# Forget attention: the softmax division moved from the probabilities into the output gate

## What is computed

```python
def fox_mixer(h, w_in, b_f, g_q, g_k, w_out):
    q, k, v, z, f_logit = jnp.split(h @ w_in, [FOX_AD, 2 * FOX_AD, 3 * FOX_AD, 4 * FOX_AD], axis=-1)
    q, k = rms_norm(q per head, g_q), rms_norm(k per head, g_k)
    F = jnp.cumsum(log_sigmoid(f_logit + b_f), axis=1)
    for i in range(S // BLK):                      # 4 blocks of 128 queries
        s = einsum('bhqd,bhkd->bhqk', q[:, :, lo:hi], k[:, :, :hi]) * scale
        s = s + F[:, :, lo:hi, None] - F[:, :, None, :hi]
        p = softmax(where(causal, s, -inf), axis=-1)
        outs.append(einsum('bhqk,bhkd->bhqd', p, v[:, :, :hi]))
    o = concatenate(outs, axis=2)
    return (o * silu(z)) @ w_out
```

## Time and profile before

| | |
|---|---|
| time, median of 3 runs | 2850.07 us (2848.01 to 2853.19) |
| span of the profiled execution | 2851.4 us |
| TensorE busy | 2608.8 us (91%) |
| VectorE busy | 1410.3 us (49%) |
| ScalarE busy | 1064.9 us (37%) |
| attention loop of the forget attention | from 788.2 to 887.2 us of the span |
| mean granted TensorE clock | 0.949 of full speed |

### The profile page before, as it was taken

How to read it: one execution, slowest core, us unless ns; L and a number is a source line. 1 busy time by engine, 2 the same in 40 slices (tenths; PEclk the granted TensorE clock), 3 DMA queues, 4 the chain that set the end, 5 groups by cost and what they waited for, 6 DMA issues and landing times.

```text
span 2851.4 us, 33398 instructions
## 1 busy us (share of the span) xinstructions
PE 2608.8 (91%) x13262; PEld 2117.5 (74%) x13262; DVE 1410.3 (49%) x2386; ACT 1064.9 (37%) x1871; POOL 269.3 (9%) x420
## 2 busy tenths in 40 slices
PE   6889899999889989999869999999967999999998
PEld 4677777788446777787647888878845888888887
DVE  4667566554374656552244333235844665533322
ACT  3355432332353545453434222233253443322222
POOL 5233021011000023000000000001001110000000
PEclk9999999999899999999879999999987999999999
DMA  5522274265111412141102333333310000233332
GB/s 213 184 71 81 86 242 157 75 199 170 53 38 54 141 30 60 60 122 52 45 30 67 104 97 97 94 94 107 90 52 1 1 1 1 67 111 97 96 96 74
DMA packets 146229, 250.19 MB, mean 88 GB/s; under 512 B 15455, under 2 KB 65914, under 8 KB 145049
## 3 DMA queue, kind: packets, MB, share of 16 engines
q1 hardware_dynamic: 129008, 198.08, 22.2%
q0 software_dynamic: 14816, 48.31, 5.1%
q10 hardware_dynamic: 2249, 1.65, 0.2%
HBM read 245.84 MB, written 5.30 MB: 88 GB/s over the span
## 4 chain that ended last, share of the span: by engine, by line
PE 77%; ACT 8%; DVE 8%; DMA 4%; issue 2%; POOL 0%; SPq 0%; DVEq 0%; ACTq 0%
PE PS L218 20%; PE PS L219 19%; PE PS L220 19%; PE PS L985 2%; ACT tmp L752 1%; PE PS L2313 1%; PE PS L2316 1%; DMA hT_b<-in_w_mod 1%; DVE x L808 1%; PE PS L2323 1%; PE PS L1760 1%; PE PS L2326 1%; PE PS L1445 1%; ACT w_hi L203 1%; PE PS L1744 1%
## 5 line engine op out<-in xcount | busy, mean ns | idle before, releaser
L210 DVE TENSOR_TENSOR w_lo<-w_raw,w_hi 128x1024 fp32r<-128x1024 f32 (+1 forms) x344 | 412.4, 1206 | 783.5 <-ACT w_hi L203 782.3
L203 ACT ACTIVATE w_hi<-w_raw 128x1024 fp32r<-128x1024 f32 (+1 forms) x344 | 356.8, 1045 | 1041.4 <-DMA w_raw<-in_ffn_w_gate_up 311.8
L218 PE MATMUL PS<-hT_hi,w_hi 128*128 128x512 f32 (+1 forms) x1728 | 662.6, 383 | 20.8 <-DVE hT_lo L820 12.7
L219 PE MATMUL PS<-hT_lo,w_hi 128*128 128x512 f32 (+1 forms) x1728 | 654.0, 378 | 0.0
L220 PE MATMUL PS<-hT_hi,w_lo 128*128 128x512 f32 (+1 forms) x1728 | 653.6, 378 | 0.0
L218 PEld LDWEIGHTS PS<-hT_hi,w_hi 128*128 128x128 f32 x1728 | 332.0, 192 | 84.7 <-issue 17.5
L220 PEld LDWEIGHTS PS<-hT_hi,w_lo 128*128 128x128 f32 x1728 | 331.9, 192 | 59.6
L219 PEld LDWEIGHTS PS<-hT_lo,w_hi 128*128 128x128 f32 x1728 | 332.5, 192 | 56.2 <-issue 0.2
L218 PE MATMUL PS<-w_hi,hT_hi 128*128 128x512 f32 (+1 forms) x704 | 290.3, 412 | 31.3 <-ACT gla_szT L1054 8.2
L219 PE MATMUL PS<-w_lo,hT_hi 128*128 128x512 f32 (+1 forms) x704 | 279.0, 396 | 0.0
L220 PE MATMUL PS<-w_hi,hT_lo 128*128 128x512 f32 (+1 forms) x704 | 277.9, 395 | 0.0
(11 more groups left out here) (564 smaller groups left out, 3479.8 us busy)
## 6 DMA issues: line engine op xcount, KB each, us to landing
w_raw<-in_ffn_w_gate_up SPq DMA_DIRECT2D x176, 256.0 KB, 3.1
mraw<-in_w_mod POOLq DMA_DIRECT2D x160, 256.0 KB, 4.0
w_raw<-in_gla_w_in SPq DMA_DIRECT2D x48, 512.0 KB, 4.7
w_raw<-in_ffn_w_down SPq DMA_DIRECT2D x44, 512.0 KB, 3.7
w_raw<-in_fox_w_in SPq DMA_DIRECT2D x32, 512.0 KB, 4.2
w_raw<-in_sgu_w_in SPq DMA_DIRECT2D x24, 512.0 KB, 4.9
w_raw<-in_dn_w_in SPq DMA_DIRECT2D x24, 512.0 KB, 3.6
w_raw<-in_gla_w_out SPq DMA_DIRECT2D x16, 512.0 KB, 4.7
```

Source lines behind the costliest of these rows:

```text
L203: nc.scalar.activation(w_hi[:, n % NS, :, 0:m], w_raw[:, n % NS, :, 0:m], ACT.Copy).then_inc(w_hidone, 1)
L210: nc.vector.tensor_tensor(w_lo[:, n % NS, :, 0:m], w_raw[:, n % NS, :, 0:m], w_hi[:, n % NS, :, 0:m].bitcast(F32), ALU.subtract).then_inc( ...
L218: nc.tensor.matmul(o, l_hi, r_hi, start=start, stop=False)
L219: nc.tensor.matmul(o, l_hi, r_lo, start=False, stop=False)
```

## The change

The probabilities are no longer divided by their row sums. The exponential writes its row sums into `r.den`, a column for each of the pair's eight units. `scale` goes; `turn` waits for the exponential itself. After a pair's last exponential VectorE inverts all eight sums at once (`invert`). TensorE gets a new step `shares`: eight matmuls of a reciprocal column, broadcast to 64 columns, with the identity, which put the reciprocals of both heads as rows into bank 7. `gate` has a new first operation, which multiplies this bank into `r.szT`, and a new wait for `q.row`. `shares(k)` stands between `values` and `turn` in the step t = 1 of the next pair (u % 8 == 2), and `gate(k)` behind the reduction of the unit with u % 8 == 3, both for the pair before; the last pair's stand behind the loop. The semaphore `f1` is renamed `row`, and the counts of other layers that share `scl` are adapted.

```diff
                 def turn(u):
                     h, t = units[u]
-                    t_.wait_ge(q.scl, u + 1)
+                    t_.wait_ge(q.ex, u + 1)
...
+                def shares(k):
+                    t_.wait_ge(q.scl, k + 1)
+                    if k:
+                        t_.wait_ge(q.os, os_at + k)
+                    for t in range(TT):
+                        for e2 in range(2):
+                            at = 2 * t + e2
+                            mm = t_.matmul(PS[FD * e2:FD * e2 + FD, 7, t * P:(t + 1) * P],
+                                           r.rd[:, k % 2, at:at + 1].to_broadcast([P, FD]), ident[:], start=True, stop=True)
+                    mm.then_inc(q.row, 1)
+
                 scores(0)
                 for u in range(0, len(units) + 2, 2):
                     if u + 2 < len(units):
                         scores(u + 2)
                     if u >= 2:
                         values(u - 2)
+                    if u % 8 == 2 and u > 8:
+                        shares(u // 8 - 1)
                     if u < len(units):
                         turn(u)
                         turn(u + 1)
+                shares(NP - 1)
                 t_.wait_ge(q.os, os_at + KT)
...
-                    a.activation(p, p, ACT.Exp, scale=-1.0, bias=r.st[:, u % 3, 0:1], accum_out=r.st[:, u % 3, 1:2]).then_inc(q.ex, 1)
+                    a.activation(p, p, ACT.Exp, scale=-1.0, bias=r.st[:, u % 3, :],
+                                 accum_out=r.den[:, u // 8 % 2, u % 8:u % 8 + 1]).then_inc(q.ex, 1)
...
-                def scale(u):
-                    h, t = units[u]
-                    v.wait_ge(q.ex, u + 1)
-                    then_dve(v.reciprocal(r.st[:, u % 3, 2:3], r.st[:, u % 3, 1:2]))
-                    p = pb(u)[:, 0:(t + 1) * P]
-                    v.tensor_scalar(p, p, r.st[:, u % 3, 2:3], None, ALU.mult).then_inc(q.scl, 1)
-                    if t == TT - 1 and h % 2 and h >= 3:
-                        gate(h // 2 - 1)
+                def invert(k):
+                    v.wait_ge(q.ex, 8 * k + 8)
+                    v.reciprocal(r.rd[:, k % 2, :], r.den[:, k % 2, :]).then_inc(q.scl, 1)
 
                 def gate(k):
+                    v.wait_ge(q.row, k + 1)
+                    then_dve(v.tensor_tensor(r.szT[:, k, :], PS[:, 7, :], r.szT[:, k, :], ALU.mult))
                     v.wait_ge(q.pv, 2 * TT * (k + 1))
                     then_dve(v.tensor_tensor(hf[:, k % 2, :], PS[:, 5 + k % 2, :], r.szT[:, k, :], ALU.mult))
                     then_dve(v.tensor_copy(hT_hi[:, k, :], hf[:, k % 2, :]))
...
-                                           scalar=-NEG, op0=ALU.add, op1=ALU.min, accum_out=r.st[:, u % 3, 0:1]).then_inc(q.ttr, 1)
-                    if u >= 1:
-                        scale(u - 1)
-                scale(len(units) - 1)
+                                           scalar=-NEG, op0=ALU.add, op1=ALU.min, accum_out=r.st[:, u % 3, :]).then_inc(q.ttr, 1)
+                    if u % 8 == 1 and u > 8:
+                        invert(u // 8 - 1)
+                    if u % 8 == 3 and u > 8:
+                        gate(u // 8 - 1)
+                invert(NP - 1)
                 gate(NP - 1)
```

More of the change, by code:

```diff
@@ L1427, in program @@
         su = sig("su", "sc ttr ex scl pt pts pv po")
-        fox_s = sig("fox", "cols lz f1 F_done flat FR0 FR1 FR2 FR3 cm cmb bones")
+        fox_s = sig("fox", "cols lz row F_done flat FR0 FR1 FR2 FR3 cm cmb bones")
         def norm_heads(base, n_tiles, per, bank, banks, sums, sq, tile, gain, rows_at, spread):
@@ L1485, in fox_layer @@
                        mask=([P, P], BF16), unit=([P, P], BF16), sums=([P, 4 * FH],), gains=([P, 8],),
-                       st=([P, 3, 4],))
+                       st=([P, 3, 1],), den=([P, 2, 8],), rd=([P, 2, 8],))
             r.F = r.FR[0:FH, 3, :]
@@ L1661, in dve @@
                 then_dve(v.tensor_tensor(r.F, r.FR[0:FH, 0, :], r.F, ALU.subtract))
-                v.memset(r.FR[0:FH, 1, :], 1.0).then_inc(q.f1, 1)
-                v.wait_ge(q.f1, 1)
+                then_dve(v.memset(r.FR[0:FH, 1, :], 1.0))
                 v.tensor_tensor_scan(r.F, r.FR[0:FH, 1, :], r.F, 0.0, ALU.mult, ALU.add).then_inc(q.F_done, 1)
@@ L1914, in att_layer @@
             NU = len(units)
-            soft = softmax_units(units + mu, FH * TT, FH * TT, 0, Group(P=r.P, PT=r.PT, st=None))
+            soft = softmax_units(units + mu, FH * TT, FH // 2, 0, Group(P=r.P, PT=r.PT, st=None))
             FILL_AT = {}
@@ L2236, in dn_layer @@
             UN = FH * TT + AH * TT + 2 * MH * TT
-            B = Group(xm=UN, pc=UN, xe=UN, te=UN, tm=UN, ym=UN, ve=0, sd=FH * TT + 2 * MH * TT,
+            B = Group(xm=UN, pc=UN, xe=UN, te=UN, tm=UN, ym=UN, ve=0, sd=FH // 2 + 2 * MH * TT,
                                 rm=0, vm=0, sm=AH // 2, rr=AH // 2, os=KT * (DEPTH + 1), kte=0)
@@ L2280, in dn_layer @@
             mu = memory_units(m_)
-            mem = softmax_units(mu, FH * TT + AH * TT + MH * TT, FH * TT + MH * TT, 8, Group(P=m_.P, PT=m_.PT, st=None))
+            mem = softmax_units(mu, FH * TT + AH * TT + MH * TT, FH // 2 + MH * TT, 8, Group(P=m_.P, PT=m_.PT, st=None))
             def load():
```

## The result

| | before | after |
|---|---|---|
| time, median | 2849.04 us (4 runs, 2839.27 to 2853.19) | 2871.38 us (4 runs, 2868.53 to 2879.89) |
| ratio | | 1.0079, 95% interval 1.0051 to 1.0107 |
| span of the profiled execution | 2851.4 us | 2866.7 us |
| loop, first scores to output projection | 788.18 to 887.21, 99.0 us | 783.01 to 908.09, 125.1 us |
| VectorE busy | 1410.3 us | 1387.6 us |

A forecast was written before the change was run, and what follows sets the result against it. It took TensorE and VectorE as both near full in the loop, a pair taking 11.46 us. Seven longer pairs (20.1), the first pair (-0.7) and the end (+1.6) sum to +21.0 us, so 2871.1, range 2865 to 2881.

The forecast's parts named there:

- The hold: In the loop, `gate` waits for `shares` and delays the reduction that scores of t = 3 need: 2.87 us longer, seven pairs.
- Shares: On TensorE in step t = 1, sixteen records without free time: 0.88 us a pair, bounds 0.88 and 1.34.
- The gain of the scaling: Turns of t = 0 and t = 1 no longer wait for VectorE's scaling: 0.73 us a pair saved.
- The first pair: At the loop's start, the first pair has no gate and keeps the gain of 0.73 us.
- The end: Behind the loop, `shares` (0.88) and one more gate operation (0.72) start the output projection 1.6 us later.
- The clock: TensorE's clock in the loop was forecast to stay at 1.00 throughout.
- rival 1: The clock falls in TensorE's new idle stretch, 1.2 us a fall; seven falls give 2879.5, three 2874.7; chance 0.20.
- The rest: Everything behind the changed loop was forecast to be shifted as a whole.
- The sum: Over the kernel, 20.1 - 0.7 + 1.6 = +21.0 us, giving a time of 2871.1.
- Rivals 2 to 5: Dearer `shares` 2874.8 (0.07); gate off the path 2852 (0.06); faster 2846 to 2842 (0.03); smaller hold 2857 to 2864 (0.09).
- rival 4: `shares` fall into TensorE's idle time and the gate into VectorE's, leaving only the gain: 2846 to 2842; chance 0.03.

The follow-up runs named there:

- late gate: The changed kernel with only VectorE's gate moved back to where the kernel before had it: 2847.0 us, ratio 0.9993 to the kernel before.
- halves apart: The changed kernel with `shares` doing four matmuls into the lower half of the partitions, then four into the upper, instead of alternating: 2890.91 us (1 run).
- hole filled: The changed kernel plus seven dummy identity matmuls where TensorE waits for the reduction behind the gate: 2870.09 us, ratio 1.0067 to the kernel before.
- shares in idle time: The late gate kernel with `shares` also moved between scores and values of step t = 3: 2839.93 us, ratio 0.9962 to the kernel before.

## Why the prediction was right

The time was forecast at 2871.1 and measured at 2871.38, and the mechanism that the forecast named, the hold, is what the runs show. But that the two numbers are so near is luck: errors in the other terms cancelled (see the last point). Point by point:

- **The hold.** Right in mechanism and size. From the turns of t = 0 the forecast had `gate` at 2.83, the reduction at 5.34, the scores at 6.03, the turns of t = 2 at 7.89; the trace has 2.79, 5.31, 5.92, 7.78. The late gate takes it away whole. The steps t = 2 and t = 3 took 812.34 - 805.91 = 6.43 us, 6.44 before, so they stayed, as forecast.
- **Shares.** 0.88 forecast, 0.88 measured by doubling them. The forecast's upper bound of 1.34, read off a group that does one half after the other, was too low for that order: it takes 1.53. The sentence of the Trainium skill (TensorE: Matmul & The Clock Gate, Part 3: Packing small matmuls) that weight loads run beside a matmul only where row groups differ would have meant 2.2 us and more; sixteen loads with all rows in use took 1.05 us, and 1.53 with the halves apart. So the trace disagrees with that sentence in both orders. The same section of the Trainium skill also lets a load run ahead into the background weight buffer, so the prediction took the page more strictly than it is written.
- **The gain of the scaling.** 0.73 forecast, 0.76 measured, and no more: in step t = 3 the values of the late gate kernel wait 0.93 us for ScalarE.
- **The first pair.** Mis-sized: from the loop's start to the turns of t = 0 of pair 1 it took 15.1 us instead of 17.2, a gain of 2.1 where 0.7 stood in the sum. By the windows at the loop's start, shown above, the clock comes back to 1.00 some 6.6 us after the loop's start, 10.2 before. All eight profiled executions without the scaling have this first pair (14.8 to 15.2 us), the two with it don't (17.0 and 17.2). The forecast had taken the gain of 0.73 from a pair at full clock.
- **The end.** 1.6 forecast; the late gate kernel, at full clock, has 14.83 us there against 13.17 before, +1.66.
- **The clock.** This is the step that failed. The forecast took 1.00 throughout and gave the falls, its rival 1, a chance of 0.20. They came, in four of six pairs and in the last, and cost 3.9 us in the six (0.74 + 1.16 + 0.73 + 1.30) and some 3 more behind (from the turns of t = 0 of the last pair to the output projection 20.8 us, 17.6 in the kernel with the hole filled). A fall was priced at 1.2 us and cost 0.7 to 1.8. With them the loop grew by 26.1 and not by 21.0.
- **The rest.** "What comes later is shifted as a whole" was wrong too: in both profiles of the changed kernel the two layers behind the forget attention were 4.0 and 4.6 us shorter than before, nearly all of it in the dilated attention.
- **The sum.** At full clock the loop would have grown by some 19 us, not 21, because of the first pair (1.3 more gained) and because a pair grew by 2.75 instead of 2.87. The falls added 7 and the layers behind took off 4: 22, beside a difference of the medians of 22.3. These errors (-2, +7, -4) have no common cause that a run shows.

Rivals 2 to 5 are out: `shares` cost what the values' shape said, the gate was in the path, the hold was not smaller by 1 us or more, and nothing was faster. But rival 4 was right on one point: such a division can be had faster than the scaling, if both new steps are put where their engines wait. That is the kernel with shares in idle time, 0.38% below the kernel before.

## What to carry to other kernels

Work that is taken off a busy engine gains only where that engine ended a wait; here it was 0.76 us of a pair though VectorE lost sixteen instructions. What a change adds must be placed by who is queued behind it: the same gate costs 2.64 us behind one reduction and nothing four microseconds later. And a hole of 1.5 us between TensorE's matmuls can cost more than itself, because the clock can fall behind it: 0.7 to 1.8 us on top in seven of the twelve pairs measured here.

## What was not expected of the hardware

- Filling a hole of TensorE with seven useless matmuls shortened the loop by 6.0 us: the granted clock was 1.00 instead of 0.92 over the six pairs.
- In the changed kernel, without the waits for the scaling, the clock came back to 1.00 after 6.6 us of the loop instead of 10.2, and the first pair got 2.1 us shorter. All eight profiled executions without the scaling agree.
- Sixteen matmul records of 64 columns take 1.05 us when they alternate between the two halves of the partitions and 1.53 us when they don't.
- An untouched layer 320 us behind the loop was 3.5 us shorter in both profiles of the changed kernel, at a granted clock of 0.90 and 0.89 instead of 0.88.
